# Layout transposes by DMA, summed probabilities before the denominator, and a planner that knows one more resource: a hybrid attention and gating layer

## The reference

```python
h = rmsnorm(x, norm_g)
proj = h @ w_in + b_in                                 # 1024 -> 2816 columns
q, k, v, z_a, u, v_s, z_s = split(proj)                # 512 128 128 512 512 512 512
attn = banded_sink_attention(q, k, v, sinks) * silu(z_a)
    # 8 query heads, 2 key heads, window of 128 keys, blocks of 128 queries:
    # block n sees the keys of blocks n-1 and n; p = exp(s); out = p @ v / (sum(p) + exp(sink))
u, v_s = gelu(u), gelu(v_s)
sgu = u * (W_masked @ layernorm(v_s) + b_s) * silu(z_s)   # in chunks of 128 positions
out = rmsnorm(x + concat(attn, sgu) @ w_out + b_out, final_norm_g)
```

## Time and profile before

| | |
|---|---|
| time, median of 3 runs | 573.43 us (571.85 to 592.07) |
| the profiled execution's own time | 572.77 us |
| its span, first to last instruction, slowest core | 571.2 us (eight cores: 566.9 to 571.2) |
| busy in the span | PE 509.7, DVE 356.5, ACT 338.9, POOL 257.4 us |
| DMA | 66.85 MB, 117 GB/s over the span |

### The profile page before, as it was taken

How to read it: one execution, slowest core, us unless ns; L and a number is a source line. 1 busy time by engine, 2 the same in 40 slices (tenths; PEclk the granted TensorE clock), 3 DMA queues, 4 the chain that set the end, 5 groups by cost and what they waited for, 6 DMA issues and landing times.

```text
span 571.2 us, 9533 instructions; the slowest of 8 cores (566.9 to 571.2 us)
## 1 busy us (share of the span) xinstructions
PE 509.7 (89%) x3106; PEld 236.5 (41%) x3106; DVE 356.5 (62%) x458; ACT 338.9 (59%) x576; POOL 257.4 (45%) x283
## 2 busy tenths in 40 slices
PE   1898699999997989999899989999899989999961
PEld 1365244443443435343354444443354444443420
DVE  2766597575767593567637685475736486375763
ACT  4235765757684756558577574748568476347531
POOL 2013598271367164441536356361454537171572
PEclk9999979999999999999999999999999999999987
DMA  7999990520233042503404043221512023100351
GB/s 226 324 338 310 317 185 8 149 75 0 111 112 110 39 148 73 175 12 93 165 38 149 1 149 110 111 76 38 179 42 74 2 102 120 73 2 19 129 218 76
DMA packets 19200, 66.85 MB, mean 117 GB/s; under 512 B 2256, under 2 KB 2384, under 8 KB 19152
## 3 DMA queue, kind: packets, MB, share of 16 engines
q1 hardware_dynamic: 17856, 64.11, 33.6%
q0 software_dynamic: 1152, 2.10, 2.4%
q10 hardware_dynamic: 144, 0.05, 0.1%
HBM read 51.56 MB, written 16.78 MB: 120 GB/s over the span
## 4 chain that ended last, share of the span: by engine, by line
PE 64%; issue 12%; DVE 9%; ACT 6%; POOL 5%; DMA 2%; POOLq 0%; DVEq 0%; SPq 0%; ACTq 0%
PE pp L498 32%; PE pp L702 14%; PE pp L552 4%; PE pp L655 3%; PE pp L523 3%; PE pp L628 2%; PE pp L659 2%; DMA xa<-x 2%; ACT LR L668 2%; PE pp L598 2%; DVE xe L707 1%; DVE vs_f L557 1%; PE pp L537 1%; PE pp L482 1%; POOL LR L674 1%
## 5 line engine op out<-in xcount | busy, mean ns | idle before, releaser
L498 PE MATMUL pp<-xT,w_fm 128*128 128x512 bf16 x1088 | 245.7, 382 | 7.2 <-DVE xe L707 2.0
L498 PEld LDWEIGHTS pp<-xT,w_fm 128*128 128x128 bf16 x1088 | 104.5, 98 | 139.5 <-issue 20.1
L702 PE MATMUL pp<-w_out_bf,mixT 128*128 128x512 bf16 x512 | 121.8, 383 | 9.4 <-DVE mixT L678 6.4
L688 POOL TENSOR_TENSOR xe<-xe,bout_sb 128x1024 f32<-128x1024 f32 x32 | 80.9, 2532 | 14.7 <-DMA xe<-x 14.6
L702 PEld LDWEIGHTS pp<-w_out_bf,mixT 128*128 128x128 bf16 x512 | 46.3, 98 | 72.3 <-issue 26.3
L674 POOL TENSOR_TENSOR LR<-LR,zaT 128x512 f32<-128x512 f32 x32 | 40.9, 1278 | 75.9 <-ACT LR L672 75.8
L707 DVE TENSOR_TENSOR xe<-pp,xe 128x512 f32<-128x512 f32 x64 | 43.6, 687 | 49.7 <-PE pp L702 46.3
L633 ACT ACTIVATE PT<-pp 128x1024 bf16<-128x1024 f32 x63 | 62.7, 1030 | 6.2 <-PE pp L628 6.2
L716 DVE SCALAR_TENSOR_TENSOR xe<-xe,st_fr,gf_sb 128x1024 f32<-128x1024 f32 x32 | 48.7, 1522 | 27.1 <-POOL st_fr L714 26.7
L646 DVE TENSOR_TENSOR PT<-PT,pack_b_sb 128x1024 bf16<-128x1024 bf16 x58 | 54.0, 940 | 6.7 <-ACT PT L633 5.7
L668 ACT ACTIVATE LR<-pp,esink 128x128 f32<-128x128 f32 x128 | 36.4, 367 | 35.3 <-PE pp L659 35.2
(11 more groups left out here) (60 smaller groups left out, 593.5 us busy)
## 6 DMA issues: line engine op xcount, KB each, us to landing
xa<-x SPq DMA_DIRECT2D x32, 512.0 KB, 6.4
xe<-x SPq DMA_DIRECT2D x32, 512.0 KB, 3.8
out<-xe SPq DMA_DIRECT2D x32, 512.0 KB, 2.7
xe<-w_in SPq DMA_DIRECT2D x12, 512.0 KB, 12.4
mixT<-w_in SPq DMA_DIRECT2D x10, 512.0 KB, 14.7
w_out_bf<-w_out POOLq DMA_DIRECT2D x8, 256.0 KB, 9.4
LR<-sgu_wT SPq DMA_DIRECT2D x1, 512.0 KB, 17.0
bout_sb<-bout_bc SPq DMA_DIRECT2D x1, 512.0 KB, 18.3
```

The lines of the kernel that those rows point to most:

```text
L498: ins = e.matmul(bank(h), lhsT=w_fm[:, FM.index(cb), k, :], rhs=xT[:, xb, k, :], start=(k == 0), stop=(k == 7))
L688: G.op("pool", lambda e: e.tensor_tensor(out=xe[:, s, :], in0=xe[:, s, :], in1=bout[:], op=ALU.add), reads=["c_bout"], writes=[("xe", s, 0 ...
L702: ins = e.matmul(bank(h), lhsT=mixT[:, mb, ec, tt * 128:(tt + 1) * 128], rhs=w_out[:, ec, hf * 512:(hf + 1) * 512], start=(ec == 0), stop= ...
```

## The change

- **Transposes.** From supertile 2 on (24 of the 32 tiles) the transposition of a scaled tile is one DMA on the SP queue, SBUF to SBUF, from `xn` into `xT`. The eight PE transposes and the copy out of PSUM of these tiles are gone.
- **Denominators.** For every block but the first (31 of 32) DVE adds the two masked halves of `PT` into a new buffer `PC`, and the ones product reads that sum: two products of 512 columns in place of four. `mmpv` waits for `PC`.
- **x(1).** The four tiles of supertile 1 are loaded after the weight blocks 5 to 8 (before: after 13, 15, 17 and 19), and each of the blocks 6 to 9 waits in the planner for that load to be placed. x(2) is placed after the last weight block.
- **Planner.** Operations marked `port` may not overlap in the planner's time when one is on DVE and the other on POOL; some costs are changed; `uT*zsT` and `LR*zaT` may now go to DVE or POOL.
- Two reads or writes are added to the graph (`vsl`, `Cmat`) that only order operations.

```diff
+            return max(t, port[0]) if o.port and e in ("dve", "pool") else t
...
-                    est = max(free[e], o.nready)
+                    est = when(o, e)
...
+            if o.port and e in ("dve", "pool"):
+                port[0] = free[e]
...
+        PC = sb("PC", [128, 2, 1024], BF16)
...
         def load_xa(st, tt):
-            after = [w_op[13 + 2 * tt]] if st == 1 else ()
+            after = [w_op[X1_AFTER[tt] - 1]] if st == 1 else [w_op[NCB - 1]] if st == 2 else ()   # X1_AFTER = (6, 7, 8, 9)
...
+            if st == 1:
+                w_op[X1_AFTER[tt]].after += (o,)
...
         def transpose_x(st, tt):
+            xb = st % 2
+            if st > 1:
+                G.op("sp", lambda e: e.dma_start_transpose(out=xT[:, xb, :, tt * 128:(tt + 1) * 128], in_=xn[:, tt % 3, :]),
+                     reads=[("xn", tt % 3)], writes=[("xT", xb, tt)], cost=1.2, dsem=d_xt[tt], kb=512, prio=st - 0.8 + 0.04 * tt)
+                return
...
-                G.op("pool", lambda e, jj=jj: e.tensor_tensor(out=uT[:, jj, :], in0=uT[:, jj, :], in1=zsT[:, jj, :], op=ALU.mult),
-                     reads=[("uT", jj), ("zsT", jj)], writes=[("uT", jj)], cost=1.27, prio=v0)
+                G.op({"dve": (0.36, fu), "pool": (1.27, fu)}, None, reads=[("uT", jj), ("zsT", jj)], writes=[("uT", jj)], prio=v0, port=True)
...
                 for g in range(2):
-                    for i, kb in enumerate(kbs):
-                        ins = e.matmul(bank(hd)[g * 64:(g + 1) * 64, :], lhsT=ones64[:, :], rhs=PT[:, p2, kb, g * 512:(g + 1) * 512],
-                                       start=(i == 0), stop=(i == len(kbs) - 1))
+                    ins = e.matmul(bank(hd)[g * 64:(g + 1) * 64, :], lhsT=ones64[:, :],
+                                   rhs=(PC[:, p2, :] if n else PT[:, p2, 1, :])[:, g * 512:(g + 1) * 512], start=True, stop=True)
...
+            if n:
+                G.op("dve", lambda e: e.tensor_tensor(out=PC[:, p2, :], in0=PT[:, p2, 0, :], in1=PT[:, p2, 1, :], op=ALU.add),
+                     reads=[("PT", p2, 0), ("PT", p2, 1)], writes=[("PC", p2)], cost=0.66, prio=v0 - 0.5, port=True)
...
+            G.op({"dve": (0.69, fz), "pool": (1.19, fz)}, None, reads=[("LR", lb)] + [("zaT", c) for c in range(4)],
+                 writes=[("LR", lb)], prio=v0 - 0.5, port=True)
```

More of the change, by code:

```diff
@@ L53 @@
     __slots__ = ("alts", "deps", "alloc", "uses", "prio", "phase", "gate", "mode", "dsem", "kb", "n", "left", "outs",
-                 "eng", "fn", "fin", "index", "dval", "nready", "final", "after")
+                 "eng", "fn", "fin", "index", "dval", "nready", "final", "after", "port")
     def __init__(self):
@@ L68, in op @@
     def op(self, eng, fn, reads=(), writes=(), cost=0.1, prio=0.0, alloc=(), uses=(), phase=None, gate=None, mode=None,
-           dsem=None, kb=0, final=False, after=()):
+           dsem=None, kb=0, final=False, after=(), port=False):
         o = Op()
@@ L134, in run, with when @@
         mode = [None]
+        port = [0.0]
+        def when(o, e):
+            t = max(free[e], o.nready)
+            return max(t, port[0]) if o.port and e in ("dve", "pool") else t
         def now_ready(o):
@@ L193, in run @@
                         mine = est + o.alts[e][0]
[L194 removed]
+                        if any(when(o, x) + c < mine - 1e-9 for x, (c, _) in o.alts.items() if x != e):
                             continue
@@ L399, in build_program @@
         d_st = [sem(f"d_st{i}") for i in range(4)]
+        d_xt = [sem(f"d_xt{i}") for i in range(4)]
         d_wo = [sem(f"d_wo{i}") for i in range(8)]
@@ L601, in mix_part @@
                 v0 = st - 0.12 + 0.01 * jj
-                G.op("pe", mmg, reads=[("vln", pc) for pc in range(4)] + ["WT"], cost=0.45, alloc=[h], prio=v0 - 5, mode="col")
+                G.op("pe", mmg, reads=[("vln", pc) for pc in range(4)] + ["WT", ("Cmat", jj)], cost=0.45, alloc=[h], prio=v0 - 5, mode="col")
                 sb_ = jj % 2
-                G.op("pool", lambda e, jj=jj: e.tensor_tensor(out=uT[:, jj, :], in0=uT[:, jj, :], in1=zsT[:, jj, :], op=ALU.mult),
-                     reads=[("uT", jj), ("zsT", jj)], writes=[("uT", jj)], cost=1.27, prio=v0)
+                fu = lambda e, jj=jj: e.tensor_tensor(out=uT[:, jj, :], in0=uT[:, jj, :], in1=zsT[:, jj, :], op=ALU.mult)
+                G.op({"dve": (0.36, fu), "pool": (1.27, fu)}, None, reads=[("uT", jj), ("zsT", jj)], writes=[("uT", jj)], prio=v0, port=True)
                 G.op("dve", lambda e, jj=jj, h=h, sb_=sb_: e.scalar_tensor_tensor(
@@ L688, in load_xe @@
             G.op("pool", lambda e: e.tensor_tensor(out=xe[:, s, :], in0=xe[:, s, :], in1=bout[:], op=ALU.add),
-                 reads=["c_bout"], writes=[("xe", s, 0), ("xe", s, 1)], cost=2.6, prio=st + 0.6 + 0.1 * s)
+                 reads=["c_bout"], writes=[("xe", s, 0), ("xe", s, 1)], cost=2.6, prio=st + 0.6 + 0.1 * s, port=True)
         def out_tile(n):
```

46 lines of the change are left out of this document (23 added, 23 removed).

## The result

The change makes the kernel faster: 535.78 us median of 4 runs (535.13 to 536.34) against 572.64 for the kernel before in the same rounds, a ratio of 0.936 with a 95% interval of 0.934 to 0.939. The forecast was 548 with a range of 539 to 567: right in its direction, too small in its size, and the range missed by 3 us. The profiled execution took 536.34 us.

What follows compares the result with a forecast made beforehand. PE was taken to bound the kernel, 95% busy from 120 to 505 us. The sum was 572.8 - 12.0 (transposes) - 7.1 (denominators) - 5 (planner) = 548.7, rounded to 548 us, range 539 to 567.

Steps and rivals of the forecast that it cites:

- Transposes, -12.0: On PE, nearly all in the steady stretch: 24 transposes removed at 0.5 us each, -12.0 us.
- The 0 for what replaces them: DMA transposes landing after 3.5 us, hidden by 3.6 us of DVE work before the q block: 0, at worst +20 us.
- the bound of 7: DMA transposes on SP's queue: each lands after at most 7 us.
- the 7.7 at which all gain was to be gone: Late-transpose rival: landing from 7.7 us on in six supertiles takes all gain; 601 us at 12.4; chance 0.07.
- Denominators, -7.1: On PE: two ones products instead of four in 31 blocks, 0.23 us saved each, -7.1 us.
- The first rival: DVE's `PC` sums before `mmpv` take PE's gain back, half of 31 exposed: +14.6, 563 us; sign `PC` first releaser; chance 0.19.
- Head, 0: Start of the program: gating wait and low clock against lost filler and earlier loads; bounds -8.9 and +6.3, taken as 0.
- The planner's part, -5: PE's 19.4 us of steady waits on DVE shrink by a quarter, -5 us; bounds 0 and -19.4.
- a mean of the mask product still at 0.94: DVE's mask product: a mean duration staying at 0.94 us would show that the port rule changes nothing.
- rival 2: In the planner: the port rule changes nothing, waits stay at 19.4 and the -5 falls away: 553 us; chance 0.17.
- The rule against the change: DVE products and POOL instructions reading SBUF exclude each other; 83 new products cost DVE 20.6 us, held by idle time.
- The end: End of the program: it keeps its chain, 0 us.

Runs made afterwards that it cites:

- 2: Changed kernel with all 32 tiles transposed on PE again and copied out of PSUM; all else stays: 550.80 us, ratio 0.961 to the kernel before.
- 9: Kernel before with only the DMA transposes and `PC` sums; old costs, no port rule, no choice of engine, old x(1): 556.60 us, ratio 0.973.
- 1: Changed kernel with the planner's port rule taken out; all else stays: 539.73 us, ratio 0.943 to the kernel before.
- 10: Changed kernel with x(1) loaded in its old places, four loads later among the weights: 535.29 us, ratio 0.937 to the kernel before.
- 5: Kernel before with the whole planner's part alone: new costs, port rule, choice of engine, two orderings; PE work and x(1) as before: 555.01 us, ratio 0.970.
- 4: Changed kernel with `uT*zsT` and `LR*zaT` allowed on POOL only; port rule stays: 543.96 us, ratio 0.951 to the kernel before.
- 6: Kernel before with the planner's new costs, two orderings and choice of engine, without the port rule: 569.38 us, ratio 0.996.
- 7: Kernel before with the planner's new costs, two orderings and port rule, both product groups on POOL only: 556.74 us, ratio 0.973.
- 8: Kernel before with only the planner's new costs and two orderings, no port rule, no choice of engine: 607.06 us, ratio 1.061.
- 3: Changed kernel with four ones products per block back and no `PC` sum; all else stays: 552.22 us, ratio 0.965 to the kernel before.

## Why the prediction was right or wrong

**Transposes, -12.0: right.** 24 x 0.5 against 13.0 on core 1, and 15.0 when they go back (2), PE's own part 12.4. The 0 for what replaces them came out too, but not by its working. The median landing of 3.6 us is the 3.5 that was taken, yet a q block reads all four tiles of a supertile, and in five of the six supertiles the fourth lands after 7.4 to 9.9 us (core 1), above the bound of 7 and, in all but one, above the 7.7 at which all gain was to be gone. PE waits for none of them, because the cover was larger than 3.6: at the nearest place, supertile 7, it is 7.8 us, and there all four land within 3.5. The closest call on core 1 is supertile 4:

```profile
240.41 4.75 SPq L493 DMA_TRANSPOSE xT<-xn  x1
249.80 1.90 PE L517 MATMUL pp<-xT,w_fm 128*128 128x512 bf16 x8
```

This transpose lands 8.6 us after its issue, at 249.0, and PE starts on the tile at 249.8. That both errors cancelled, with 0.8 us to spare, is luck.

**Denominators, -7.1: right.** 6.8, and DVE's sums take 756 ns in the mean where 0.69 to 0.94 was taken. `PC` is no releaser worth a row. The first rival, that the sums take the gain back, fell: even without the planner's part the steady waits don't grow (9). Its sign, `PC` first in the list, shows only without the port rule (1), with 1.4 us.

**Head, 0: right** in its sum: PE waits 1.6 us more before 120 us, and the old places of x(1) give the same time (10). The wait changed its place, from the gating product to a v_s block. That a gain and a loss cancelled, as the bounds have it, isn't shown.

**The planner's part, -5: the step that failed.** "DVE's added load works against it, so I take a quarter." The waits from 120 us on fell by 13.5 of 15.7 us on core 1, not by a quarter, and the planner's part as a whole is worth 17.5 us alone (5; 11.1 of it are steady waits, 16.5 to 5.4) and 20.8 beside the other parts (9). The bound below (-19.4) had it; the choice within the bounds was wrong. The reason given was load, and load was not what made PE wait: DVE rose from 62% to 72% of the steady stretch (core 1), and PE's waits went from 16.5 to 2.3 us. Nor was it POOL's load, by 4. What is left is which instruction stands where in DVE's and POOL's lists; the planner's part changes that. Neither its rule nor its choice is the only way to it: with the choice and without the rule 5.0 us of idle PE are left (6), with the rule and without the choice 9.2 (7), with neither 27.7 (8). The prediction had the right row: every releaser in the earlier trace rows was DVE, and DVE was idle for 37% of the time, so it was late without being short of time.

The other half of that step, that the rule must shorten the long instructions to have an effect, was only half right. In 5 against 6 it does (mean of the mask product 762 and 1074 ns, core 1), in the kernel after against 1 it doesn't (898 and 890 on their slowest cores), and the steady waits are small in all four; in 7 the mean is as long as before (951 for 925, core 1), and they are nearly halved. So "a mean of the mask product still at 0.94" was a false sign of rival 2: the mean counts long instructions that nobody waits for. Rival 2 itself, that the port rule changes nothing, fell: the rule is worth 3.9 us beside all the rest (1), 14.4 in 5 against 6 and 50.3 in 7 against 8. The 14.4 are mostly the price of one product of 11.20 us, the 50.3 of one of 12.71 and of 18.5 us of steady waits; both products stand in lists made with the new costs and without the rule, and before the change the longest was 2.85.

**The rule against the change.** The Trainium skill, "SBUF — State Buffer", section "Who interferes with whom", lets such a product and a GpSimd instruction that reads SBUF shut each other out. The trace of experiment 6 agrees, and more strongly than the row of before could tell: 11.20 us for a product of 0.68, under four additions of 9.27 us in a row, where the earlier trace rows had 2.85 as the worst. By that rule the 83 new products looked like a burden; in the kernel after none of them releases PE in the list shown above. What held the long product in the 1.36 us before the first addition, beside POOL's DMA issues, stays open.

**The end.** Not in the sum: the wait ahead of the last output block lost 2.4 us, the chain behind it grew by 1.7 on core 1 and by 2.8 on the cores of the two pages (15.0 for 12.2).

What stays open: why the new costs and the two orderings alone are worse than the old ones by 35 us. Experiment 8 shows the long product in the head and 27.7 us of idle PE later, most of it behind DVE's addition `xe` (8.3 and 7.8 us in its two largest rows), but not which of the changed costs, or which ordering, puts them there. How much of the gain the rule or the choice would bring with the old costs was not run either. And in 3, 4 and 8 the planner writes another head each time, so that a few us there belong to no part by itself.

## What to carry to other kernels

When the engine that bounds the kernel waits for one that is not busy, price the waits as a matter of order, and ask for the whole of them first: here 14 of 16.5 us went while the late engine got busier. A DMA that replaces work of the bounding engine cost nothing here where the DMA engines had room just before it, and 9.0 us for four tiles where they were full: place it by the DMA share right ahead of it, not by the average of a long stretch, and compare the latest landing, not the median, with the cover. In a list planned ahead, taking one operation or one choice back moved the head by several us (3, 4), so an undo test is read stretch by stretch and not by its total.

## What the runs showed of the hardware that was not expected

- A DVE product of two SBUF inputs (0.68 us) lasted 11.20 us beside four POOL additions in a row (experiment 6) and 12.71 us beside a mixed run of POOL's products and additions (8): it ended 0.57 and 0.56 us after the last of them, not after the first.
- A DMA transpose of a 128x1024 bf16 tile holds SP's queue for 1.25 us (median) and lands after 3.6 (3.0 to 9.9); with the DMA engines at a share of 1.19 in the 10 us before, it held the queue for 9.7 us and landed after 26.2. Queue q1 carried 25,344 packets more than before (43200 for 17856; 1056 for a transpose) and its share rose from 33.6 to 44.5%, without a wait of PE.
- On core 0 some 50 records of products were missing, and its rows read as 7.6 us of idle PE in the steady stretch, where the cores with the full count had 2.3 to 4.2.
